# First group's gates by token, branch and output blocks held in the gather buffers, tile 0 ahead of tile 1, embedding rows read in order

## What is computed

```python
proj = x @ w_in                                  # ua, va, q, k, v, r, gk_low, g_a, g_b
y_a = chunk_spatial_gate(gelu(ua), LN(gelu(va)), w_s, b_s)
o, S_new = gla(q, k, v, log_a, S0)               # 4 heads, state 128 x 256 each
y_b = silu(r) * rms(o) * gla_norm_g
m = sigmoid(g_a) * (y_a @ w_br_a) + sigmoid(g_b) * (y_b @ w_br_b)
x1 = LN(alpha * x + m @ w_o)
# PEER: 8 heads, 2 x 128 product keys, top 16 of 128 x 128 experts for every token and head
q = norm(x1 @ w_q); s = q @ keys; idx, gate = softmax(top16(s1 + s2))
w = gate * gelu(u_tab[idx] @ x1);  y = sum(w * v_tab[idx])
x2 = LN(alpha * x1 + y)
x3 = x2 + (p @ w_pe) * sigmoid(x2 @ w_pg)
```

## Time and profile before

| | us |
|---|---|
| median of 3 runs | 1989.66 (1983.47 to 1993.34) |
| profiled execution | 1995.63 |
| its span, first to last instruction | 1993.5 |

### The profile page before, as it was taken

One profiled execution on the slowest core, in us unless ns is written; L12 is line 12 of the kernel. 1 busy time (PEld: TensorE's weight loads), 2 busy tenths in 40 slices (PEclk: granted clock), 3 DMA queues, 4 the chain that ended last, 5 costly groups with the idle time before them and its releaser, 6 DMA issues.

```text
span 1993.5 us, 19824 instructions
## 1 busy us (share of the span) xinstructions
PE 1443.4 (72%) x6736; PEld 906.0 (45%) x6736; DVE 1164.6 (58%) x2987; ACT 406.0 (20%) x813; POOL 990.9 (50%) x1052
## 2 busy tenths in 40 slices
PE   9999996689888779889886788246542436674546
PEld 7888885576554347556653455013220101131113
DVE  1110112776777657685667755687678877866511
ACT  2310200224232222131111212121122211121000
POOL 0000000336665556665555655677666677767760
PEclk9999998799997779998898899667676665687588
DMA  6344442689999999999999899999999999999992
GB/s 255 119 146 148 148 149 85 251 305 412 410 411 412 389 377 405 410 412 412 408 407 377 327 380 374 399 406 398 405 379 364 374 409 409 409 396 399 409 387 87
DMA packets 188404, 675.81 MB, mean 339 GB/s; under 512 B 36329, under 2 KB 38505, under 8 KB 174482
## 3 DMA queue, kind: packets, MB, share of 16 engines
q0 software_dynamic: 149760, 545.33, 69.9%
q1 hardware_dynamic: 38546, 129.23, 17.4%
HBM read 667.07 MB, written 7.41 MB: 338 GB/s over the span
## 4 chain that ended last, share of the span: by engine, by line
PE 43%; DMA 25%; DVE 16%; POOL 7%; issue 5%; ACT 2%; SPq 1%; DVEq 0%; PEldq 0%; POOLq 0%
PE PJ L1383 13%; DMA at<-in_v_tab,idxV 13%; PE PJ L1281 10%; PE Y L1433 7%; DVE at L1164 6%; DMA at<-in_u_tab,idx 5%; PE PJ L1288 4%; POOL at L637 4%; POOL at L646 3%; PE PJ L1267 3%; DMA at<-in_w_q 2%; DMA at<-in_p_t 1%; DMA at<-in_state 1%; PE PJ L1342 1%; DMA out_st_s<-at 1%
## 5 line engine op out<-in xcount | busy, mean ns | idle before, releaser
L637 POOL DMA_INDIRECT at<-in_u_tab,idx x512 | 486.8, 951 | 642.3 <-DVEq L1147 351.5
L1164 DVE CUSTOM_DVE_ANT_0 at<-at,XD 128x1024 f32<-128x1024 f32 x512 | 614.6, 1216 | 200.4 <-DMA at<-in_u_tab,idx 187.5
L646 POOL DMA_INDIRECT at<-in_v_tab,idxV x512 | 487.2, 952 | 319.4 <-PE Y L1433 181.4
L1433 PE MATMUL Y<-at,at 128*32 128x512 f32 x2048 | 344.3, 792 | 317.5 <-DMA at<-in_v_tab,idxV 306.5
L1383 PE MATMUL PJ<-at,at 128*128 128x256 f32 (+1 forms) x1792 | 416.5, 392 | 2.1 <-issue 1.1
L1383 PEld LDWEIGHTS PJ<-at,at 128*128 128x128 f32 x1792 | 345.0, 195 | 78.1 <-issue 19.4
L1433 PEld LDWEIGHTS Y<-at,at 128*32 128x32 f32 x2048 | 73.4, 130 | 504.1 <-issue 488.8
L1281 PE MATMUL PJ<-at,at 128*128 128x256 f32 (+2 forms) x960 | 240.5, 412 | 41.8 <-DMA at<-in_w_q 28.5
L1281 PEld LDWEIGHTS PJ<-at,at 128*128 128x128 f32 (+2 forms) x960 | 179.0, 190 | 104.0 <-DMA at<-in_w_q 31.2
L1267 PE MATMUL PJ<-at,at 128*128 128x256 f32 (+1 forms) x640 | 143.6, 383 | 0.0
L1267 PEld LDWEIGHTS PJ<-at,at 128*128 128x128 f32 (+1 forms) x640 | 107.6, 171 | 38.6 <-issue 12.6
(11 more groups left out here) (208 smaller groups left out, 1333.4 us busy)
## 6 DMA issues: line engine op xcount, KB each, us to landing
at<-in_w_blk SPq DMA_DIRECT2D x72, 1024.0 KB, 7.9
at<-in_w_q SPq DMA_DIRECT2D x16, 1024.0 KB, 8.7
at<-in_w_o SPq DMA_DIRECT2D x8, 1024.0 KB, 6.5
at<-in_u_tab,idx POOLq DMA_INDIRECT x512, 11.8
at<-in_v_tab,idxV POOLq DMA_INDIRECT x512, 11.1
at<-in_state SPq DMA_DIRECT2D x4, 1024.0 KB, 8.2
out_st_s<-at SPq DMA_DIRECT2D x4, 1024.0 KB, 7.1
at<-in_w_pg SPq DMA_DIRECT2D x2, 2048.0 KB, 13.2
```

The source lines that it names most:

```text
L637: pool.indirect_dma_start(ubuf[slot], None, u_tab, bass.IndirectOffsetOnAxis(rows_of, 0)).then_inc(u_in[slot], 16)
L646: pool.indirect_dma_start(vbuf[slot], None, v_tab, bass.IndirectOffsetOnAxis(rows_of, 0)).then_inc(v_in[slot], 16)
L1164: v.tensor_tensor_reduce(out=t, in0=t, in1=XD[:, :], scale=1.0, scalar=0.0, op0=ALU.mult, op1=ALU.add, accum_out=hraw[:, n % 2, k:k + 1]). ...
L1433: last = mm(Y[32 * c:32 * c + 32, s, :], wpadV[d // PAIR % 2][:, g, :], vbuf[slot][:, 512 * s:512 * s + 512], start=False, stop=final)
```

## The change

Five things are done.

- In group 0 the gates and branches (`gb`, `brb`, `ga`, `bra`) are computed by token: jobs named "gb of", "brb of", "ga of", "bra of", each of 256 channels for one tile, results in `gb_of` and `ga_of`. Since m is now laid out by token, new jobs `mt` turn it (4 transposes each, two jobs for a tile, copied by ACT into `rT`), and `wo` reads `rT`.
- The four `bra` blocks and four `wo` blocks of group 0 leave the ring. They are loaded into the space of the 7 u and 9 v buffers (`held`), one at each `v` and `va` job of tile 1, and each has a semaphore of its own. POOL waits, before its first gather, for the last `bra` job of tile 1, and before step 1, where v gathers begin, for the last `wo` job.
- The order after the mixers: `bra`, `mt`, `wo`, `x1`, `t1` and the first two `wq` jobs of tile 0 stand ahead of tile 1's `bra`, whose jobs are woven with the first two choices. Tile 1's `z` jobs are woven into tile 0's chain. The last two `wo` jobs of tile 1, its `x1` and `t1` and three `wq` jobs stand in slots 1 to 12 of step -1. What is left is spread from step -1 slot 13.
- The second choice has only parts 4 to 6 left in step -1 (slots 0, 2, 4), the third starts at slot 14 instead of 9.
- `load_p` becomes one DMA for a tile into a second buffer `p_read`, in the tokens' order; ACT copies it into `pT` in the other order (`order`), after which the next tile's load is issued.

```diff
-        out += ot[j0] + gb[:1] + ot[j1] + gb[1:]
-    out += columns(g, "brb")
+        gate_b = [e for i in range(4) for e in natural(0, "gb of", i)]
+        out += ot[j0] + gate_b[:1] + ot[j1] + gate_b[1:]
+    out += columns(g, "brb") if g else [e for i in range(4) for e in natural(0, "brb of", i)]
...
-    out += weave(columns(g, "ga"), [("job", g, "z", half, j) for j in TILES[g] for half in range(2)])
+    if g == 0:
+        return out + weave([e for i in range(4) for e in natural(0, "ga of", i)], turn(0, "z", j0))
+    out += weave(columns(g, "ga"), [e for j in TILES[g] for e in turn(g, "z", j)])
...
-            put(choice(0, 1), -1, (1, 2, 2, 3, 4, 5, 6, 7, 8))
+            put(choice(0, 1)[6:], -1, (0, 2, 4))
         elif r == 2:
-            put(choice(0, 2), -1, (9, 10, 11, 12, 13, 14, 16, 18, 20))
+            put(choice(0, 2), -1, (14, 15, 16, 17, 18, 19, 21, 23, 25))
...
-    wo, wq = out_rows(0), queries(0)
-    out = mixers(0) + wo[:7] + x1[0][:1] + wo[7:] + x1[0][1:] + turn(0, "t1", 0) + wq[:1]
-    out += choice(0, 0)
-    out += x1[1] + turn(0, "t1", 1) + wq[1:2]
+    bra, wo = ([[("job", 0, name, i, j) for i in range(4)] for j in TILES[0]] for name in ("bra of", "wo"))
+    z, mt = turn(0, "z", 1), [turn(0, "mt", j) for j in TILES[0]]
+    wq = [("job", 0, "wq", i + a, j) for i in range(0, PH, 2) for j in TILES[0] for a in range(2)]
+    first, second = choice(0, 0), choice(0, 1)
+    out = mixers(0) + bra[0] + mt[0][:1] + z[:1] + mt[0][1:] + wo[0] + x1[0][:1] + z[1:] + x1[0][1:] + bra[1][:1]
+    out += turn(0, "t1", 0) + wq[:1] + first[:2] + wq[1:2] + first[2:4]
+    out += bra[1][1:2] + second[:2] + first[4:5] + second[2:3] + bra[1][2:3] + first[5:6] + bra[1][3:]
+    out += first[6:7] + mt[1] + first[7:] + second[3:4] + wo[1][:1] + second[4:5] + wo[1][1:2] + second[5:6]
...
-    behind = spread_over(wq[2:] + mixers(1) + second + wq2[:1], (-1, 0), (13, 6))
+    behind = spread_over(wq[5:] + mixers(1) + close + wq2[:1], (-1, 13), (13, 6))
     behind.update(spread_over(wq2[1:], (13, 10), (15, 15)))
+    behind.setdefault((END, 10), []).append(("order", NT - 1))
     for j, at in REST_AT.items():
+        behind.setdefault((at, 1), []).append(("order", j))
...
+    for k, e in zip((1, 3, 5, 7, 8, 9, 10, 11, 12), wo[1][2:] + x1[1] + turn(0, "t1", 1) + wq[2:5]):
+        behind.setdefault((-1, k), []).append(e)
...
+HELD_BLOCKS = [("bra", i) for i in range(4)] + [("wo", i, half) for i in range(2) for half in range(2)]
+HELD_FROM = {("job", 0, name, i, 1): 4 * n + i for n, name in enumerate(("v", "va")) for i in range(4)}
...
-                for c in range(2):
-                    natural_order = p_t[:, c, cols(j)].rearrange("p (j b i) -> p b j i", j=4, b=4)
-                    for b in range(4):
-                        sp.dma_start(pT[:, c, 32 * b:32 * b + 32].rearrange("p (j i) -> p j i", j=4),
-                                     natural_order[:, b]).then_inc(pt_in, 16)
+                sp.dma_start(p_read, p_t[:, :, cols(j)]).then_inc(pt_in, 16)
...
+                if n == -1:
+                    pool.wait_ge(pj_done, JOB["job", 0, "bra of", 3, 1] + 1)
+                if n == 1:
+                    pool.wait_ge(pj_done, JOB["job", 0, "wo", 3, 1] + 1)
...
+            def order(j):
+
+                p, i = rows(j), REST[j]
+                act.wait_ge(pt_in, PT_IN[j])
+                if i:
+                    act.wait_ge(pj_done, JOB["job", 1, "pe", 3, list(REST)[i - 1]] + 1)
...
+                for c in range(2):
+                    last = act.activation(pT[:, c, :].rearrange("p (b j i) -> p b j i", b=4, j=4),
+                                          p_read[:, c, :].rearrange("p (j b i) -> p b j i", j=4, b=4), ACT.Copy)
+                last.then_inc(pt_ok, 1)
...
+                elif name in ("gb of", "brb of", "ga of", "bra of"):
+                    src = {"brb of": rT, "bra of": uaT}.get(name, xT)
...
+                    for k in range(KC):
+                        last = mm(out[:, 0:BC], src[:, k, local(c)], w[:, k, :], start=k == 0, stop=k == KC - 1)
+                elif name == "mt":
+                    pe.wait_ge(m_ok, 4 * c + 2 * i + 2)
```

More of the change, by code:

```diff
@@ L289 @@
 REST = numbers(e[4] for e in PLAN if e[0] == "job" and e[2:4] == ("pg", 3))
-PT_IN = {j: sum(16 if i == NT else 128 for i in list(REST)[:REST[j] + 1]) for j in REST}
+PT_IN = {j: 16 * (REST[j] + 1) for j in REST}
 U_SAMPLE, V_SAMPLE = (SAMPLE_DOTS_AT + 1) * TOPK, (SAMPLE_SUMS_AT - 1) * TOPK
@@ L388, in decoder_step @@
         bsrow = take(G * 128)[0:1]
+        O_HELD = place[0]
+        held = [at(O_HELD + 2048 * i, KC, BC) for i in range(4)]
+        held_wide = [at(O_HELD + 2048 * i, KC // 2, 512) for i in range(4, 8)]
+        assert 2048 * len(HELD) <= (UB + VB) * D
         ubuf = [take(D) for _ in range(UB)]
@@ L402, in decoder_step @@
         Ep, Em = at(O_L + H * CW, H, 128), at(O_L + H * CW + 512, H, 128)
+        ga_of = [at(O_L + D * j, D) for j in range(2)]
+        gb_of = [at(O_QK, D), Q[1].rearrange("p a b -> p (a b)")[:, 0:D]]
         o_at = O_L + H * CW
@@ L500, in load_block @@
                 b = STREAM[s]
+                kind = b[1].split()[0]
                 if s >= RING:
@@ L545, in _ @@
             for e in PLAN:
+                if e in HELD_FROM:
+                    m = HELD_FROM[e]
+                    b = HELD_BLOCKS[m]
+                    if b[0] == "wo":
+                        sp.dma_start(held_wide[m % 4], w_o[b[1]][:, 4 * b[2]:4 * b[2] + 4, :]).then_inc(held_in[m], 16)
+                    else:
+                        sp.dma_start(held[m], w_blk[BLOCKS.index(f"bra{b[1]}")]).then_inc(held_in[m], 16)
                 if e[0] == "job":
@@ L852, in _ @@
                     spread(*args)
+                elif what == "order":
+                    order(*args)
                 elif what == "sample dot" and args[0] == S - 1:
@@ L1075, in combine @@
                     v.tensor_tensor(t, t, b, ALU.add).then_inc(m_ok, 1)
+                elif name == "brb of":
+                    v.wait_ge(pj_act, ACT_DONE["job", 0, "gb of", i, c])
+                    t = gb_of[c][:, BC * i:BC * i + BC]
+                    v.tensor_tensor(t, t, src[:, 0:BC], ALU.mult).then_inc(pj_dve, 1)
+                elif name == "bra of":
+                    v.wait_ge(pj_act, ACT_DONE["job", 0, "ga of", i, c])
+                    t, b = (x[c][:, BC * i:BC * i + BC] for x in (ga_of, gb_of))
+                    v.tensor_tensor(t, t, src[:, 0:BC], ALU.mult).then_inc(pj_dve, 1)
+                    v.wait_ge(pj_dve, n)
+                    v.tensor_tensor(t, t, b, ALU.add).then_inc(m_ok, 1)
                 elif name == "wo":
@@ L1267, in job @@
                         last = mm(out[0:p, 0:BC], xT[:, k, local(c)], w[:, k, :], start=k == 0, stop=k == KC - 1)
+                elif name in ("gb of", "brb of", "ga of", "bra of"):
+                    src = {"brb of": rT, "bra of": uaT}.get(name, xT)
+                    if name == "brb of":
+                        pe.wait_ge(pj_dve, DVE_DONE["job", 0, "ot", 1, c])
+                    elif name == "bra of":
+                        pe.wait_ge(pj_dve, DVE_DONE["job", 0, "z", 1, c])
+                    w = held[held_block("bra", i)] if name == "bra of" else ring[block_of(g, name, i)]
+                    for k in range(KC):
+                        last = mm(out[:, 0:BC], src[:, k, local(c)], w[:, k, :], start=k == 0, stop=k == KC - 1)
+                elif name == "mt":
+                    pe.wait_ge(m_ok, 4 * c + 2 * i + 2)
+                    for a in range(4):
+                        k = 4 * i + a
+                        last = nc.tensor.transpose(out[:, a * 128:a * 128 + 128], ga_of[c][:, k * 128:(k + 1) * 128], ident[:, :])
                 elif name in ("wo", "wq"):
                     p = rows(c)
-                    if name == "wo":
-                        pe.wait_ge(m_ok, KC * (g + 1))
+                    if name == "wo" and g:
+                        pe.wait_ge(m_ok, 4 * len(TILES[0]) + KC)
+                    elif name == "wo":
+                        pe.wait_ge(pj_act, ACT_DONE["job", 0, "mt", 1, c])
                     else:
                         pe.wait_ge(pj_act, ACT_DONE["job", g, "t1", 1, c])
-                    src, sample_q = gaT if name == "wo" else x1T, (name, c) == ("wq", NT)
+                    src, sample_q = (gaT if g else rT) if name == "wo" else x1T, (name, c) == ("wq", NT)
                     if sample_q:
```

48 lines of the change are left out of this document (34 added, 14 removed).

## The result

The changed kernel takes 1976.46 us, the median of 13 runs (1972.08 to 1983.39), beside 1991.80 for 13 runs of the kernel before: ratio 0.9927, 95% interval 0.9914 to 0.9940. By the ratio that is 14.5 us faster (12 to 17), by the medians 15.3. 1976.46 lies inside the predicted range, near its upper end, with the sign as forecast; the gain was forecast at 31 us. Its profiled execution took 1976.46 us, with a span of 1974.7. The profiled execution of the kernel before, 1995.63, is 3.8 us above the median of its 13 runs, so a difference between the two profiles (19.2 us) is larger than the gain.

The account below looks back on a forecast made before the run. PE's jobs bound the time up to the first gather, bytes through the DMA engines after it. Head 16.5, embedding rows 5.4 and tail 9 sum to 31 us, off the median 1989.7: 1959 us, range 1940 to 1978.

Parts of the forecast that it names:

- the order's own timing: From `bra` to tile 1's layernorm: `bra` starts at 257.1, first gather at 331.8, tile 1 normalised at about 361.
- nothing for the held blocks and the form by token: Loads during `v` and `va`: the eight held blocks cost nothing; `mt` jobs add 5 us, half on the path and counted.
- the stream of gathers is 20 us ahead and PE 1 us ... I charge 4 us of idle DMA: First gather to first v gather: gathers lead by 20 us, PE's second group by 1; idle DMA costs 4 us.
- The head: Gain from putting tile 0 ahead of tile 1, up to the gathers: 16.5 us, between 1.4 and 22.
- PE's spare time: PE's 16.4 us of waits for v rows, after the second group starts, take up its denser work by 600.
- The embedding rows: Middle, `p_t` loads in tokens' order: 512-byte instead of 32-byte runs give 5.4 us, between 0 and 7.
- The tail: End of the kernel: `embed` without a wait lets the sums follow the gathers, 9 us, between 0 and 12.
- 1949: Rival for the whole kernel: the whole lead is kept and other DMA gaps shrink, 41 us gained; chance 0.15.
- Packed PE is the bound: Rival after the first gather: denser PE work bounds the rest, gain 1.4 + 5.4 + 9 = 16 us, 1974; chance 0.17.
- It does not do what it says: Rival at the head: held loads delay the ring's blocks 21 us, first gather unmoved; 14 us gained, 1975; chance 0.06.
- The tail did not stay at the low clock: Rival at the end: sparse PE keeps the gate's matmuls at 1.2 GHz, 10 us lost, 1969; chance 0.07.
- The slower case: Between 340 and 435 PE stays cold; second group 62 us late, net 30 us slower, 2020; chance 0.04.

Follow-up runs that it names:

- Both edits together: Changed kernel with group 0's fourth and fifth `w_q` blocks loaded into free space and tile 1's layernorm moved to slot 0 of step -1: 1954.69 us, ratio 0.9810.
- the light kernels: Half of the matmuls left out in group 1's by-channel, `v` and `va` jobs: changed kernel 1977.42 us, changed kernel with the old order of tiles 1982.11 us.
- the one with the `w_q` blocks aside: Changed kernel with group 0's fourth and fifth `w_q` blocks loaded into free space outside the ring: 2049.29 us (ratio 0.9878), again 1964.17 us (0.9853).

## Why the prediction was right or wrong

**Right: the bound, and the order's own timing.** Two regimes, jobs on PE and then bytes, with DMA full from the tenth slice. The first gather, the layernorm of tile 1 and the start of `bra` came within 3 us of the forecast, and from `bra` to `wo` of tile 0, with the `mt` jobs, it took 4.9 us for 5.6.

**Not refuted, and not settled: nothing for the held blocks and the form by token.** With the old order they move the v gathers of step 16 by about 1 us, but by the times 4 us, give or take 5, could be theirs.

**Wrong, and most of the miss: "the stream of gathers is 20 us ahead and PE 1 us ... I charge 4 us of idle DMA".** The head was to bring 16.5 and the order brings 7.4. Two readings were at fault. First, a first gather 21 us early is a lead of 21 us only if the stream then runs at the DMA engines' rate. It runs at what seven u buffers and DVE's dots allow, and the dots stand in DVE's order behind queries that come from `wq` jobs, which wait for `w_q` blocks. I had this chain in the earlier trace rows, had counted its 22.7 us of waits, low clock and turns on PE as unchanged, and saw one DVE wait of about 13 us. PE's 14 jobs took 77.1 us from 361.28, 28.4 more than their work; the block waits alone grew from 9.1 to 15.6. Of DVE's waits there are four, of 15.77, 2.46, 6.52 and 8.03, and POOL stands 15.92, 9.33 and 9.58 us behind three of them. The u gathers show it round by round: the first of the second sixteen goes out 33.7 us earlier than before, of the third 18.6, of the fourth 9.7. In 380 to 400 the rate falls to 175 GB/s. By the windows from 380 to 450 the idle DMA costs 5.7 + 3.0 us more than before, not 4.

Second, I let PE's spare time of the earlier trace rows repay what was lost. Bytes that were not moved while the engines had room were not moved later either: the lead is 12.0 us at step 1 and 10.1 at step 16. PE's waits for v rows, which I expected near zero, are 5.8 and 6.6 us in 500 to 600, as before (5.7 and 6.6); only the 4.1 of 440 to 500 is gone. So the spare time was not used up, and using it would have moved no bytes.

Both edits together test this reading. They take no work away and leave the first gather where it is or later, and they bring 21.1 us by keeping the DMA engines busy between 350 and 450.

**The embedding rows: mechanism right, and in the middle 5.4 was 3.4 to 6.1.** The windows at 388 GB/s are gone: the 19 windows of 10 us of after between 1260 and 1450 read 404 to 416. The rate from 1250 to 1450 is 409 against 402, 1.4 MB or 3.4 us; the gathers say 4.1 between steps 16 and 20, 3.4 for the part alone, and 6.1 when the runs are put back. The Trainium skill, "DMA: Bandwidth & Descriptors", Specifications, gives 512 B as the smallest transfer for line rate; the windows agree, with 388 GB/s beside 32-byte runs and 404 to 416 beside 512-byte runs. On the first chip no gain could be measured. Together with the tail this part was forecast at 14.4 us; made alone it brought 3.9 (1.6 to 8.6), so the two terms together were too large beyond the noise.

**The tail: mechanism right, 9 was about 5 and less elsewhere.** The sign was a distance from the last u gather to the end of the last sums shorter by 8 to 11 us. It is 6.0 shorter, 4.4 in the second execution of the changed kernel, 2.9 with the embedding rows alone, and 2.8 with the 32-byte runs put back, so that much of it needs only the early load and not the longer runs. The last gather was forecast 11.1 us early besides the lead, and it is 10.7 (24.6 less 13.9). The step that failed is the backlog behind it. I had its bytes end 3.8 us after its issue and landed 0.8 later; it landed 7.7 us after its issue (1940.3), and the last sums followed at the low clock, 3.5, as charged. That is 3.1 us, and the slower gate 1.1 more (17.01 against 15.88), for which I had put some 1. At 1890 and 1896 POOL waits 4.12 and 1.39 us for PE's sums, and the rate is 349 and 367 GB/s in the windows from 1890 and 1900, a dip that the forecast did not have.

**What adds up and what doesn't.** Between the two profiles it is 10.1 us at step 16, 4.1 more by step 20, 0.3 less by the last u gather, and 4.9 behind it with the gate: the 18.8 between the spans. But 3.1 us at step 16 are there with the embedding rows alone too, where the program had been the kernel before up to 1230. By the runs the order's 7.4 and the rows' 3.9 make 11.3, beside 15.3 and 17.0 by the medians in two sets. The 4 to 6 us between are not assigned by any run; the form by token with the held blocks may hold some of them.

**The other signs.** The first gather (332.50), the windows and `embed` came as written. The first v gather (432.99, not 420 to 430) and the second group (438.40, not 430 to 438) did not. DMA's share from 450 to 600 was 1.03, and tile 1 was normalised before 358.61, so two of the three signs that the forecast is wrong stayed away. The third, low clock in `wq`, showed at the first jobs after each wait: 288, 294 and 248 ns a matmul in the dense stretches that start at 361.28, 377.92 and 401.08, where warm ones take 218. The range was to take in 1949 and 1975 with 5 us of spread, which is 1944 to 1980, and was given as 1940 to 1978; the result lies in both.

**The rivals.** *Packed PE is the bound* named a time near the measured one (1974), by luck, for a reason that the light kernels refute; its 1.4 us of head is too little as well. *It does not do what it says* (1975) falls by the first gather. The tail did not stay at the low clock. The slower case did not occur: the 56 matmuls at 401.08 took 13.89 us, 248 ns each with a slow start after the wait, the granted clock from 400 to 450 was 0.90, and the second group starts at 438.40 where that case had 497.

## What to carry to other kernels

Where a stage bound by compute leads into one bound by bytes, a reordering is worth the extra bytes moved at the moment the DMA engines become full, so add up rate by time in windows up to there, and not how much earlier the first transfer starts. After moving the start of a stream, follow it for its first rounds through the slowest chain that feeds it (here `w_q` block, `wq` job, query, dots, free buffer), and price the engines' idle time in each round. Spare time on an engine that was not the bound paid nothing back here. And make each part of a change alone: two terms read off a profile, 14.4 us, were 3.9 when made alone.

## What the runs showed of the hardware

Chips differ: the same program takes 2072.19 us on one and 1992.69 or 1991.85 on another. Whether the value of an edit differs with it is not shown: the embedding rows alone measured 0.9980 to 1.0038 on the first and 0.9957 to 0.9992 on the other, and the two intervals overlap.

A dense stretch of PE does not run at one speed in every profile. Nine profiles have the new order up to the first gather, and in all of them PE works without a gap from 180 to 250. `bra` of tile 0 (64 matmuls) then took 14.05 us in three of them, among them both executions of the changed kernel, and 15.7 in the other six. Those 14.05 are 220 ns a matmul, the pace of 2.4 GHz; in the six the granted clock from 250 to 275 was 0.93, against 0.97 to 0.99 in the three, so part of the matmuls ran at 1.2 GHz. From 300 to 335 the granted clock was 1.00 in the two of the changed kernel and 0.90 to 0.95 in the rest. The first gathers of the three go out at 331.7 to 332.5, those of five of the six at 335.9 to 337.0 and that of the sixth at 334.0: some 4 us, more than several of the terms argued over here. The two programs that were profiled twice each repeated their pace (the changed kernel 14.05 both times, the one with the `w_q` blocks aside 15.7 both times), so it may belong to the program and not to the execution; no run here tells which.
